# Two first layers side by side in the TensorE array, gates beside local values, place columns and masks inside neighbouring blocks

## The reference, cut to what matters

```
def nsa_compress(k, pe, w1, w2):
    ch = k.reshape(b, n_ch, CMP_STRIDE, g, d)
    blocks = jnp.concatenate([ch[:, i:i + ncmp] for i in range(n_sub)], axis=2)
    blocks = blocks + pe[None, None, :, None, :]
    blocks = jnp.moveaxis(blocks, 3, 1).reshape(b, g, ncmp, CMP_BLOCK * d)
    return jax.nn.gelu(blocks @ w1) @ w2
...
kc = nsa_compress(kv(nkc), cmp_pe_k[l], cmp_w1_k[l], cmp_w2_k[l])
vc = nsa_compress(kv(nvc), cmp_pe_v[l], cmp_w1_v[l], cmp_w2_v[l])
gates = jnp.transpose(jax.nn.sigmoid(ngate.reshape(b, s, NSA_HEADS, 3)), (0, 2, 1, 3))
```

## Time and profile before

| | |
|---|---|
| time, 3 runs | 3281.1 to 3281.46 us, median 3281.25 us |
| profiled execution, span from its first to its last instruction | 3277.8 us (its own whole time is not given apart from the span) |
| PE busy | 3041.5 us, 93% of the span |
| DVE busy | 1445.8 us, 44% |
| ACT busy | 693.9 us, 21% |
| POOL busy | 122.2 us, 4% |
| mean granted TensorE clock | 0.954 of full speed |

### The profile page before, as it was taken

How to read it: one execution, slowest core, us unless ns; L and a number is a source line. 1 busy time by engine, 2 the same in 40 slices (tenths; PEclk the granted TensorE clock), 3 DMA queues, 4 the chain that set the end, 5 groups by cost and what they waited for, 6 DMA issues and landing times. The chain is left out here.

```text
span 3277.8 us, 38675 instructions
## 1 busy us (share of the span) xinstructions
PE 3041.5 (93%) x15110; PEld 2171.4 (66%) x15110; DVE 1445.8 (44%) x2559; ACT 693.9 (21%) x1594; POOL 122.2 (4%) x144
## 2 busy tenths in 40 slices
PE   8989998999999889988999999999889986999997
PEld 4467766888878578877688887867666634333332
DVE  3554424334353758367533354324644232333335
ACT  1311113220010643561101001114531212111111
POOL 1000000000000200000000000000100011000000
PEclk9989999999999979999999999998889997999998
DMA  9121211222221002101122322221012107999995
GB/s 377 52 78 54 75 67 69 87 100 77 93 73 68 26 27 103 52 1 65 64 91 77 108 72 77 91 92 52 1 65 77 56 11 313 423 425 422 424 424 219
DMA packets 129894, 420.48 MB, mean 128 GB/s; under 512 B 6705, under 2 KB 35778, under 8 KB 108242
## 3 DMA queue, kind: packets, MB, share of 16 engines
q1 hardware_dynamic: 121842, 379.48, 30.1%
q10 hardware_dynamic: 3024, 23.59, 1.8%
q0 software_dynamic: 4880, 15.35, 1.3%
HBM read 394.81 MB, written 23.59 MB: 128 GB/s over the span
## 5 line engine op out<-in xcount | busy, mean ns | idle before, releaser
L777 PE MATMUL bank<-arena 128*128 128x256 f32 x5152 | 1129.6, 382 | 30.5 <-issue 15.5
L777 PEld LDWEIGHTS bank<-arena 128*128 128x128 f32 x5152 | 987.1, 192 | 173.6 <-issue 23.1
L1073 PE MATMUL bank<-arena 128*128 128x256 f32 x1652 | 362.7, 382 | 10.0 <-PEq L131 3.5
L1073 PEld LDWEIGHTS bank<-arena 128*128 128x128 f32 x1652 | 316.5, 192 | 54.9 <-issue 11.3
L178 PE MATMUL bank<-arena 128*128 128x512 f32 (+7 forms) x804 | 254.1, 473 | 38.0 <-PEq L3446 11.5
L178 PEld LDWEIGHTS bank<-arena 128*128 128x128 f32 (+3 forms) x804 | 137.3, 195 | 149.0 <-issue 128.1
L425 PE MATMUL bank<-arena 128*128 128x512 f32 x384 | 167.7, 598 | 4.2 <-PEq L1685 2.0
L3886 DVE TENSOR_TENSOR arena<-arena,bank 128x512 f32<-128x512 f32 x128 | 87.7, 687 | 139.1 <-PE bank L3790 136.8
L841 DVE TENSOR_TENSOR arena<-arena 128x1024 f32<-128x1024 f32 x46 | 56.3, 1224 | 183.0 <-PE bank L777 179.5
L425 PEld LDWEIGHTS bank<-arena 128*128 128x128 f32 x384 | 73.1, 192 | 95.4 <-issue 95.4
L3790 PE MATMUL bank<-arena 128*128 128x512 f32 x256 | 123.1, 616 | 4.4 <-DVE arena L3872 4.4
(11 more groups left out here) (555 smaller groups left out, 3515.8 us busy)
## 6 DMA issues: line engine op xcount, KB each, us to landing
arena<-in_moe_w_gate_dram SPq DMA_DIRECT2D x64, 1024.0 KB, 16.4
arena<-in_moe_w_up_dram SPq DMA_DIRECT2D x64, 1024.0 KB, 18.6
arena<-in_moe_w_down_dram SPq DMA_DIRECT2D x32, 2048.0 KB, 23.9
arena<-in_w_in_dram SPq DMA_DIRECT2D x29, 2048.0 KB, 7.9
arena<-in_w_ff_dram SPq DMA_DIRECT2D x16, 2048.0 KB, 7.8
x_slots<-arena ACTq DMA_DIRECT2D x8, 2048.0 KB, 32.7
arena<-in_w_out_dram SPq DMA_DIRECT2D x8, 2048.0 KB, 7.8
arena<-in_w_gate_dram SPq DMA_DIRECT2D x11, 1024.0 KB, 5.2
```

The costliest lines, as they stand in the source:

```text
L777: last = pe.matmul(bank[:, m, :], lhsT, rhs, start=fresh and m == 0 and k == 0, stop=k == 3, skip_group_check=True)
L1073: last = pe.matmul(bank[:, m, :], x[:, k, m * P:(m + 1) * P], w[:, k, :], start=opening and m == 0 and k == 0, stop=k == w.shape[1] - 1, s ...
```

## The change

- `tokens_from` makes the local values and the gates in one product of 152 columns (128 + 24) for each 128 tokens; ACT empties both parts, a copy and a sigmoid. Before, DVE and ACT took turns with the values.
- The eight additions of place columns move into the block before, behind DVE's last bank (`after_v`). Their own block goes.
- Both first layers are one group: for each of the 16 slices a matmul into partitions 0 to 61 of a bank, and one into partitions 64 to 125 of the same bank. In the built program the pair has tiles of 128 rows by 64 columns, at columns 0 and 64 of the array. ACT takes the two gelus one after the other, and the turns of both wait for both.
- The masks, the causal pattern and the gate column are all made by POOL (`meanwhile`) in the block of the compressions. Their own block goes.
- The weight chunks of both first layers are released together.

```diff
-    groups += tokens_from(c, ("nwin", 3), xT, (128, 256), [vW[:, i, :] for i in range(NT)], last=False)
-    sigmoid_to = lambda dst: lambda act, bank, order: act.activation(dst, bank[:, 0:24], ACT.Sigmoid)
-    groups += tokens_from(c, ("nwin", 3), xT, (256, 280), None, [sigmoid_to(gates[:, i, :]) for i in range(NT)],
-                          who="a")
+
+    def values_and_gates(i):
+
+        def run(act, bank, order):
+            act.activation(vW[:, i, :], bank[:, 0:P], ACT.Copy).then_inc(order.sem, order.up())
+            act.wait_ge(order.sem, order.sent)
+            return act.activation(gates[:, i, :], bank[:, P:P + 24], ACT.Sigmoid)
+        return run
+    groups += tokens_from(c, ("nwin", 3), xT, (128, 280), None, [values_and_gates(i) for i in range(NT)], who="a")
...
+    def add_places(dve, order):
+
+        dve.wait_ge(c.signals["bank_emptied_by_vector"].sem, c.signals["bank_emptied_by_vector"].at(2))
...
+        dve.wait_ge(place_added.sem, place_added.at(8))
+    bank_groups(c, groups, meanwhile=second_weights, after_v=add_places)
...
-    groups = []
-    for n, w1 in enumerate(("cmp_w1_k_3", "cmp_w1_v_3")):
-        w = c.slot(w1)[0]
-
-        def gelu(act, bank, order, n=n):
-            return act.activation(by_block[n][0:width, :], bank[0:width, 0:256], ACT.Gelu_apprx_tanh)
-        groups.append(((w1,), product([(blocks[n][:, k, :], w[:, k, :]) for k in range(CBLOCK // 2)]), (w1,), "a",
-                       gelu))
+    rows = [slice(64 * n, 64 * n + width) for n in range(2)]
+    by_block = c.region(10, 2048, 256)
+    keys = ("cmp_w1_k_3", "cmp_w1_v_3")
+    w1 = [c.slot(key)[0] for key in keys]
+
+    def both_first_layers(pe, bank):
+        for k in range(CBLOCK // 2):
+            for n in range(2):
+                last = pe.matmul(bank[rows[n], 0:256], blocks[n][:, k, :], w1[n][:, k, :], start=k == 0,
+                                 stop=k == CBLOCK // 2 - 1)
+        return last
+
+    def gelu(act, bank, order):
+        act.activation(by_block[rows[0], :], bank[rows[0], 0:256], ACT.Gelu_apprx_tanh).then_inc(order.sem, order.up())
+        act.wait_ge(order.sem, order.sent)
+        return act.activation(by_block[rows[1], :], bank[rows[1], 0:256], ACT.Gelu_apprx_tanh)
+    groups = [(keys, both_first_layers, keys, "a", gelu)]
...
+    def masks_and_gates(pool):
+
+        pool.memset(seen, 1.0).then_inc(made.sem, made.up())
+        pool.memset(hide, 0.0).then_inc(made.sem, made.up())
+        pool.memset(causal[:, 0:S - P], 0.0).then_inc(made.sem, made.up())
+        pool.tensor_copy(causal[:, S - P:S], c.keep_le[:, :]).then_inc(made.sem, made.up())
...
+        pool.tensor_scalar(gates[:, 0, 0:24:3], gates[:, 0, 0:24:3], seen, None, ALU.mult).then_inc(made.sem, made.up())
+        pool.wait_ge(made.sem, made.at(7))
+    bank_groups(c, groups, meanwhile=masks_and_gates)
```

More of the change, by code:

```diff
@@ L2881, in second_weights @@
         pool.wait_ge(got.sem, got.at(48))
-    bank_groups(c, groups, meanwhile=second_weights)
+    blocks = compressed_blocks(c)
+    place_added = c.sig("term_added")
+    def add_places(dve, order):
+        dve.wait_ge(c.signals["bank_emptied_by_vector"].sem, c.signals["bank_emptied_by_vector"].at(2))
+        for n, (src, pe_name) in enumerate(((kC, "cmp_pe_k_3"), (vC, "cmp_pe_v_3"))):
+            for g in range(NG):
+                for m in range(2):
+                    half = slice(m * 8, m * 8 + 8)
+                    tokens = src[:, g, m * CSTRIDE:m * CSTRIDE + NCMP * CSTRIDE].rearrange(
+                        "p (n k two) -> p k n two", k=8, two=2)[:, :, :, 0]
+                    dst = blocks[n][:, half, g * NCMP:(g + 1) * NCMP]
+                    dve.tensor_tensor(dst, tokens, c.col[pe_name][:, half].unsqueeze(2).to_broadcast([P, 8, NCMP]),
+                                      ALU.add).then_inc(place_added.sem, place_added.up())
+        dve.wait_ge(place_added.sem, place_added.at(8))
+    bank_groups(c, groups, meanwhile=second_weights, after_v=add_places)
     memory = Memory(c, mem)
-    sparse_attention(c, a, w2, qT, kS, kW, kC, vC, vS, vW, gates, mixT, memory)
+    sparse_attention(c, a, w2, blocks, qT, kS, kW, vS, vW, gates, mixT, memory)
     gated_recurrence(c, a, hq, hk, hf, hv, hgate, lb, one_less, mixT, memory)
@@ L3025, in _, with compressed_blocks, sparse_attention @@
             c.load_weights(sync)
-def sparse_attention(c, a, w2, qT, kS, kW, kC, vC, vS, vW, gates, mixT, memory):
+def compressed_blocks(c):
+    return [c.region(10, n * 1024, CBLOCK // 2, NG * NCMP) for n in range(2)]
+def sparse_attention(c, a, w2, blocks, qT, kS, kW, vS, vW, gates, mixT, memory):
     nc = c.nc
@@ L3036, in sparse_attention @@
     width = NG * NCMP
[L3037 to L3057, removed]
@@ L3066, in sparse_attention, with turn_hidden, run @@
+    groups = [(keys, both_first_layers, keys, "a", gelu)]
+    def turn_hidden(n):
+        def run(pe, bank):
+            for m in range(2):
+                last = pe.transpose(bank[:, m * width:(m + 1) * width], by_block[rows[n], m * P:(m + 1) * P],
+                                    c.ident[rows[n], rows[n]])
+            return last
+        return run
     for n in range(2):
-        groups.append(((), turns(c, [by_block[n][0:width, m * P:(m + 1) * P] for m in range(2)]), (), "v",
-                       copy_to(hidden[n]), [n]))
+        groups.append(((), turn_hidden(n), (), "v", copy_to(hidden[n]), [0]))
@@ L3074, in copy_both @@
         return dve.tensor_copy(kcmp[64:128, :, :], bank[0:64, 0:width].rearrange("p (g n) -> p g n", g=NG))
-    groups.append(((), product([(w2[0][:, m, :], hidden[0][:, m, :]) for m in range(2)]), (), "v", copy_both, [2]))
+    groups.append(((), product([(w2[0][:, m, :], hidden[0][:, m, :]) for m in range(2)]), (), "v", copy_both, [1]))
     for g in range(NG):
         groups.append(((), product([(hidden[1][:, m, g * NCMP:(g + 1) * NCMP], w2[1][:, m, :]) for m in range(2)]), (),
-                       "v", copy_to(vcmp[0:NCMP, g, :]), [3]))
@@ L3079, in sparse_attention @@
-    bank_groups(c, groups)
+                       "v", copy_to(vcmp[0:NCMP, g, :]), [2]))
     hide, causal = c.region(11, ATT_WORK, NT, NCMP), c.region(11, 2048, S)
     seen = c.small[:, 112:113]
[L3083 to L3103, removed]
@@ new lines, in sparse_attention @@
+    made = c.sig("iota_made")
+    def masks_and_gates(pool):
[3 more added lines that the diff above has]
+        pool.tensor_copy(causal[:, S - P:S], c.keep_le[:, :]).then_inc(made.sem, made.up())
+        pool.wait_ge(made.sem, made.at(2))
+        pool.affine_select(out=seen, in_=seen, compare_op=ALU.is_ge, fill=0.0, base=-(CBLOCK - 1),
+                           pattern=[[0, 1]], channel_multiplier=1).then_inc(made.sem, made.up())
+        pool.affine_select(out=hide, in_=hide, compare_op=ALU.is_ge, fill=NEG, base=-(CBLOCK - 1),
+                           pattern=[[P, NT], [-CSTRIDE, NCMP]], channel_multiplier=1).then_inc(made.sem, made.up())
+        pool.wait_ge(made.sem, made.at(6))
+        pool.tensor_scalar(gates[:, 0, 0:24:3], gates[:, 0, 0:24:3], seen, None, ALU.mult).then_inc(made.sem, made.up())
+        pool.wait_ge(made.sem, made.at(7))
```

## The result

The changed kernel takes 3254.8 us (median of 4 runs, 3252.2 to 3261.8), the kernel before, on the same chip, 3281.2 (3279.8 to 3281.5). The medians are 26.4 us apart; the ratio is 0.9924 (0.76% faster), with a 95% interval of 0.9912 to 0.9936. The prediction was 3259.7 in a range from 3252 to 3267. A second series of five runs of the changed kernel gave 3253.1 (3252.2 to 3259.2) against 3280.0, ratio 0.9922 (0.9908 to 0.9935). In both series the profiled execution of the changed kernel was the fastest one (3252.2).

A forecast was written before the change was run, and what follows sets the result against it. PE, busy for 93% of the span, was taken as the bound, in a chain of blocks each ending with a meeting of all engines. -6.8 - 4.4 - 9.6 + 0.8 - 1.5 = -21.5 us from 3281.25 gave 3259.7, range 3252 to 3267.

The forecast's parts named there:

- (a): Local values and gates: one 152-column product replaces the separate 128- and 24-wide ones; net -6.8 us.
- (b): Ahead of the first layers: the block of eight additions goes, and they cost nothing in their new place; -4.4 us.
- (c): First layers side by side at full clock: 7.1 us in place of 16.7; -9.6 us, 2.7 of it slow clock.
- 13.8 us for turns: First layers: upper bound if the halves take turns, 64 records at 0.21, from 11.10 us for 53 at full clock.
- (d): Behind the first layers: gelus now follow each other, +0.43, and keys' turns and copy are no longer hidden, +0.35; together +0.8 us.
- (e): Ahead of the attention: the block of masks goes, 2.0 us become one meeting of 0.5, POOL's work is covered; -1.5 us.
- halves in turns: First layers: both halves write the same bank and take turns; +6.7 us, 3266.4; chance 0.03.
- first layers at half clock: PE starts the first layers at low clock; 2.7 us come back (3262.4), or 7 if throughout (3266.7); chance 0.06.
- The one on weight loads: First layers: each pair's weight loads stand outside the matmuls; +4.5 us, 3264.2; chance 0.03.
- the last step: From the attention's first matmul to the end of the span: 1048.7 us, as before.
- The rival of the attention's clock: Moving the attention's start changes which rounds meet the low clock; 6.1 us per fall, either way; chance 0.13 each.
- one fall fewer: In the attention, the clock falls in one round less than before; 3253.6 us; chance 0.13.

The follow-up runs named there:

- halves_in_turn: The changed kernel with the first-layer group making all 16 slices of the keys, then all 16 of the values; 3259.6 us, one run.
- halves_alone: The kernel before with only the side-by-side first layers and what hangs on them; gates, place columns and masks as before; 3270.9 us, one run.
- masks_apart: The changed kernel with the masks in a block of their own again, on POOL and DVE; 3263.1 us, one run.
- start_later: The changed kernel with a 128x1792 memset on DVE behind the compressions' last copy, to hold back the attention's start; 3261.7 us, one run.
- warm_attention: The changed kernel with one unread 512-column product each behind the attention's second, third and fourth unit, none in the block before; 3250.6 us.

## Why the prediction was right, and by how much it was not

Term by term, from the two timelines:

(a) Predicted -6.8. The last sigmoid starts at 2196.19, not 2203.16: -6.97. Groups of 152 columns are 2.07 us apart (2.11 predicted).

(b) Predicted -4.4. From the last sigmoid's start to the first layers 5.23 us became 0.65: -4.58. The additions cost nothing, with 1.7 us of cover left before the last sigmoid.

(c) Predicted -9.6. 2208.39 to 2225.08 became 2196.84 to 2204.00: -9.53. The pairs run at full clock and 0.22 us apart. It is right for the reasons given, in two parts: some 6.7 us are the halves side by side (6.1 against halves_in_turn, with its eight records in pairs), and some 2.8 the clock, beside the 2.6 that halves_alone lost by it. One figure beside the forecast was wrong. Its 13.8 us for turns was said to come from 53 records in 11.10 us, which gives 13.4; the records start 0.216 us apart, and that does give 13.8. The reading that both the 24-wide gates and the standstill had kept the clock down was argued from the earlier trace rows and is now shown from both sides. Either one suffices, by one profile of each: with (a) undone the layers take 8.50, with (b) undone 9.92. So the 2.6 us of halves_alone belong to no part alone, and the parts one by one do not add up to the whole.

(d) Predicted +0.8, measured +0.84: from the last wait for a first layer to DVE's last copy 2.02 us became 2.86.

(e) Predicted -1.5. From DVE's last copy to the attention 2.02 us became 0.33: -1.69; masks_apart gives 1.7 as well. POOL needed 1.7 us of the 10.

Sum -21.9 against -21.5 predicted. The forecast took the 3.45 us between the profile's span and the median for what lies around the span. On record this is 1.6 to 1.9 us in every run but one (masks_apart, 2.8); the rest, some 1.8 us, is that the profiled execution of before was faster than that median. As only the difference was carried over, the forecast does not suffer.

The rivals: halves in turns and first layers at half clock did not come about. The one on weight loads falls with PEld's row, 64 loads in 6.70 us beside 7.13 us of matmuls. A load of a column half is hidden beside the matmuls although there are only 0.22 us from pair to pair. The rule of the Trainium skill ("TensorE: Matmul & The Clock Gate", Part 3, The mechanism) that only other row groups let a load overlap does not describe this trace. The same section also lets a load into the background weight buffer go ahead of matmuls in flight, which would fit; the prediction left this out, and no row shows into which buffer a load goes.

What was off is the last step, "from there on the distance to the end should be 1048.7 us as before". It is 1043.3. Of the 5.8 us by which the profiled span lies under the 3256.3 expected, 5.4 are this step and 0.4 the stage; the median of the timed runs lies 4.9 under the 3259.7. The rival of the attention's clock had the mechanism, and its case with one fall fewer, 3253.6, came about in the profile: the third round takes 26.1 us, not 32.2. It was given 0.13, as the exception. Against it a first round longer by 2.3 us was not foreseen. The sensitivity was there to be read; which way it would go was not. That the extra gain went to this kernel is luck as far as the prediction goes: masks_apart, with the same work behind the stage, has the third round low again and 1048.7 us. That a fall moves with the start stays argued. start_later and masks_apart have other patterns, but each is one execution.

It was also said that the three runs of before agree within 0.36 us, and so the pattern is stable for a program. For the changed kernel this does not hold: the runs range over 9.7 us, where before has 2.9 over all runs. The granted clocks on record go with it: 0.958 in the runs up to 3254.5 us, 0.957 at 3255.1, 0.956 at 3259.2 and 0.955 at 3261.8. A mean that is lower by 0.003 is some 20 us more at the low level, and at the price of the third round before (6.1 us for 13.4) that is 9 us, an estimate. So the spread has the size of the clock's share. In which rounds or stages the executions of 3255 us and more met the low level, and why only some did, stays open, since none of them has a profile.

## What to carry to other kernels

Here two float32 matmuls with 62 output rows and 256 columns, written next to each other into partitions 0 and 64 of one bank, took the time of one; written one group after the other they took that of two. Narrow products (24 of 512 columns) and standstills of some microseconds can cost twice, as they did here, once by themselves and once by the low clock in what follows, so a part that fills or removes one should be valued with its neighbours. And where a stage of small, mutually waiting products follows, ask at what clock it starts: a few unread wide products in PE's waits took 10 us off a 43 us round here, at a price of up to 2, and left 4 us of it in the kernel's time. Differences of a few microseconds between single runs say nothing about an edit until the stretch that was edited is measured by itself.

## What the runs showed of the hardware

With the attention's start 2 us later behind a longer standstill (start_later), its fourth round, 100 us later, took 6 us more at a low clock; whether the edit or the run's own spread did it is not shown. The same program took 3252.2 to 3261.8 us, with mean granted clocks from 0.958 to 0.955. The same code ahead of the change reached the same point up to 2.8 us apart in different executions (2187.6 to 2190.4). With three unread wide products between the first scores the low stretch at the attention's start was that of a 3.2 us window row (warm_attention), without them that of a 30.3 us one. And two column halves in one PSUM bank ran at once: 64 records of 256 columns in 7.13 us, with loads of 0.14 us each hidden beside them. In the changed kernel the clock stayed low through the 30.3 us row although PE shows as busy in 30.16 of its 30.30 us, so the busy time in the profile does not tell by itself at which level the clock will be.
